# Row tiles of the first norm in groups of 2, 2, 4, 4, 4, the next group's rows between the matmul blocks, and two weight splits moved into the second norm

## The chip, the core and the metric

One core of one Trainium2 chip runs the whole kernel in one launch. The metric is the device time in microseconds (us). The engines named below are PE (TensorE, the matrix engine), DVE (VectorE), ACT (ScalarE), POOL (GpSimd) and SP (SyncE, which issues nearly all DMAs).

## The reference, cut to what matters

The reference is one decoder layer in float32 over 512 tokens of width 2048, conditioned on a vector `c`:

```python
mod = silu(c) @ w_ada + b_ada                    # 2048 -> 6 * 2048
shift1, scale1, gate1, shift2, scale2, gate2 = split(mod, 6)
h = rms_norm(x, norm1_g) * (1 + scale1) + shift1 # first norm
proj = h @ w_in                                  # retention, attention and indexer inputs
...                                              # retention heads, top-k sparse attention
x = x + gate1 * (concat(y_ret, y_dsa) @ w_out)
h = rms_norm(x, norm2_g) * (1 + scale2) + shift2 # second norm
y = square(relu(h @ w_mlp1)) @ w_mlp2            # 2048 -> 8192 -> 2048
return x + gate2 * y
```

## The kernel before

**Arithmetic.** Every float32 weight chunk is split in two: ACT writes the high part (`split_hi`, line 514), POOL subtracts it from the raw chunk and writes the low part (`split_lo`, line 739), and PE forms each product in three passes (high by high, high by low, low by high; line 1196). A split chunk lies in one of four places of `w_hi` and `w_lo`, and `split_hi` of a chunk waits until PE has used the chunk four before it. Raw weights come in units of four chunks into two slots of `raw`.

**Start.** `x` is 4 tiles of 128 tokens (1024 KB each), loaded into two places of `x_nat`. PE turns each tile (`turn_x`, 16 transposes), ACT copies the turned columns into `resid` and squares each `x` tile for the mean square (line 661). POOL takes the root, PE spreads it over the partitions (`spread`, line 1269), and DVE copies it to `rstd1` (line 842). Between its bursts PE does a few dummy matmuls (`fill`).

**Rows of the first norm.** The first norm needs scale and shift for each of the 16 row tiles (128 rows of the width 2048) of `h`. They come from `w_ada`, for which nothing is kept from call to call: for four row tiles there are 8 pieces of 1024 KB (`first_piece`, line 456; 4 pieces of scale, 4 of shift, each 128 partitions by 4 runs of 512 columns, so 2048 bytes in a run), loaded in turn into four buffers `first[0..3]`. A piece is issued on SP only when PE has used the piece four before it (`first_used`). PE multiplies each piece by the silu of `c` (`first_rows`, line 1283, 4 matmuls of 512 columns), accumulating in bank 3 of `pa`. When 8 pieces are in, ACT copies the bank to `part_rows` (`take_first`, line 520), PE sums and turns it (`sum_first`, line 1304), DVE adds the bias (line 817) and forms the gain (`fold`, line 822). Then, for each row tile: DVE writes `tmp` (line 830), ACT writes the high part of `h` (`h_high`, line 524), DVE the low part (line 834).

**Early chunks.** PE multiplies each row tile of `h` as soon as it is there with its 896 columns of `w_in` (`early_chunk`: four blocks into `pj`, one for each token tile, and three blocks into `pa`; 16 chunks in all). Groups are of four row tiles: group 0 is prepared ahead of the first chunk, and the pieces of group `cc` lie between the chunks of group `cc - 1`, none ahead of the first of them, four ahead of the second, two ahead of each of the others. The sum of group `cc` stands inside the fourth chunk, after its second block.

**SP's order.** SP works through one list: the constants, `x` tiles 0 and 1, the first four pieces, `x` tiles 2 and 3, the rest of group 0 with the four quarters of weight unit 0 (448 KB each), and then for each group 8 pieces with weight unit `cc` (1792 KB) after the fourth. A wait in this list holds back all that stands behind it.

**Second norm.** After the output projection the second norm writes 16 row tiles of `h` in the same three steps (`tmp` lies in `relu`, and the spread root stays in PSUM). PE starts `first_unit` (the first MLP unit, row tiles 0 to 7) as soon as its tiles come. ACT splits the chunks of the second MLP unit (`U_MLP + 1`) after it has written all 16 high parts.

Of the kernel before, what the change touches and what calls it, by code (L numbers as in the profile page):

```python
# [27 lines left out]
ALU = mybir.AluOpType  # L28
ACT = mybir.ActivationFunctionType

P = 128
# [68 lines left out]


def need(eng, sem, value):

    if isinstance(value, int) and value <= 0:
        return
    eng.wait_ge(sem, value)
# [20 lines left out]
def build(nc, x, vecs, b_ada, consts, w_ada, w_in, w_out, w_mlp1, w_mlp2, out):  # L127
# [21 lines left out]
    def small(name, *shape):  # L149
# [44 lines left out]

    x_nat = at("x_nat", 65536 + 16384, [P, 2, D])
    first = [at("ada_first0", 12 * 4096, [P, 2048]), at("ada_first1", 14 * 4096, [P, 2048]),
             at("ada_first2", RC + 4096, [P, 2048]), at("ada_first3", RC + 22528, [P, 2048])]
# [39 lines left out]
    x_turned, x_taken = sem("x_turned"), sem("x_taken")  # L237
    x_squared = sem("x_squared")
    rstd_spread = sem("rstd_spread")
# [117 lines left out]
    for n in range(2, ADA_PIECES):  # L357
        after = max(after, ada_place(n)[2] - 1)
        ADA_AFTER.setdefault(after, []).append(n)

    block = nc.Block()
    with block:
# [3 lines left out]
        def _(sp):  # L366
            def ada_piece(n):

                (sec, k), (b, _, freed) = divmod(n, 4), ada_place(n)
                if n == 0:  # L370
                    sp.wait_ge(first_used, 32)
# [21 lines left out]
            def load_head(k):  # L393

                g = k // 4
                if k == 0:
                    sp.wait_ge(mod_taken, 8 + ADA_SUMS)
                elif k == 1:
# [52 lines left out]
            def first_piece(cc, t):  # L451

                sec, s = divmod(t, 4)
                need(sp, first_used, 8 * cc + t - 3)
                col = D * (1 - sec) + 512 * cc
                sp.dma_start(first[t % 4][:].rearrange("p (k n) -> p k n", k=4),
                             ada_v[:, 4 * s:4 * s + 4, col:col + 512]).then_inc(first_landed[t % 4], 16)

# [6 lines left out]
            for s in range(2):  # L465
                sp.wait_ge(x_turned, 4 * s + 4)
                sp.wait_ge(x_squared, s + 1)
                sp.dma_start(x_nat[:, s, :], x[P * (s + 2):P * (s + 3), :]).then_inc(x_landed[s], 16)
            for t in range(4, 8):
                if t == 6:  # L470
                    load_quarter(0)
                first_piece(0, t)
            for j in range(1, 4):
                load_quarter(j)
            for cc in range(1, 4):
                for t in range(8):
                    if t == 4:
                        if cc == 1:
                            sp.wait_ge(x_turned, 16)
                            sp.wait_ge(x_squared, 4)  # L480
                        load_unit(cc)
                    first_piece(cc, t)
# [24 lines left out]
        def _(act):  # L507
# [8 lines left out]
            def take_first(cc):  # L516

                act.wait_ge(first_used, 8 * cc + 8)
                need(act, mod_summed, cc)
                act.activation(part_rows[:], pa[:, 3, :], ACT.Copy).then_inc(first_taken, 1)  # L520

# [133 lines left out]
            for tb in range(NB):  # L655
                if tb == 1:
                    act.wait_ge(rows_taken, 2)
                    act.activation(csilu[:, 1, :], vec[:, V_C:V_C + KT], ACT.Exp, scale=-1.0).then_inc(silu_exp, 1)
                act.wait_ge(x_landed[tb % 2], 16 * (tb // 2 + 1))
                need(act, x_squared, tb)  # L660
                act.activation(x_junk[:], x_nat[:, tb % 2, :], ACT.Square,
                               accum_out=ms[:, tb:tb + 1]).then_inc(x_squared, 1)
                for q in range(4):
                    act.wait_ge(x_turned, 4 * tb + q + 1)
                    act.activation(resid[:, 4 * q:4 * q + 4, P * tb:P * tb + P],
                                   pj[:, q, :].rearrange("p (k t) -> p k t", k=4), ACT.Copy).then_inc(x_taken, 1)
            for cc in range(4):
                for j in range(4):
                    if cc > 0 and j == 2:
                        take_first(cc)  # L670
                    split_hi(cc, j)
                    if cc == 0:
                        if j == 0:
                            take_first(0)
# [51 lines left out]

            mlp_step(0, 4)
            with act.Fori(1, STEPS - 1) as c:
# [51 lines left out]
        def _(dve):  # L780
            own = Steps(dve, dve_step)

            dve.memset(half[:], -0.5).then_inc(half_set, 1)
            own.step(dve.memset(c_wide[:], 0.0))
            dve.wait_ge(rows_turned, 1)
            dve.tensor_copy(bias_cols[:], pa[:, 0, 0:96]).then_inc(rows_taken, 1)
# [16 lines left out]
            def take_mod(n):  # L803

                col = 2 * KT + 4 * n
                dve.wait_ge(mod_summed, 4 + n + 1)
                summed = pj[:, 0, 0:4] if n in ADA_ASIDE else pa[:, 3, 0:4]
# [3 lines left out]
            def take_first_mods(cc):  # L811

                dve.wait_ge(mod_summed, cc + 1)
                sums_ = pa[:, 3, 0:8].rearrange("p (m sec) -> p sec m", sec=2)
                for sec in range(2):
                    col = KT * (1 - sec) + 4 * cc
                    dve.tensor_tensor(mod[:, col:col + 4], sums_[:, sec, :], bias_cols[:, col:col + 4],
                                      ALU.add).then_inc(mod_taken, 1)
# [17 lines left out]

            for cc in range(4):
                if cc == 0:
                    dve.wait_ge(x_squared, NB)
                    dve.tensor_scalar(ms[:, 0:NB], ms[:, 0:NB], 1.0 / D, EPS, ALU.mult, ALU.add).then_inc(ms_ready, 1)  # L840
# [4 lines left out]
                dve.wait_ge(mod_taken, 2 * cc + 2)  # L845
                fold(4 * cc, 0, KT, V_N1, 4)
                for m in range(5):
                    kt = 4 * cc + m
                    if m < 4:
                        modulate(kt, 0, resid, rstd1[:], tmp1, 0, t_ready, h_hi, h_ready, 0)  # L850
# [151 lines left out]
            def ada_add(n):  # L1002
# [5 lines left out]
                if n % 4 == 0:  # L1008
                    dve.wait_ge(mod_summed, max(4, 3 + n // 4))
                for i in range(4):  # L1010
# [10 lines left out]
            for q in range(Q_WO):  # L1021
# [35 lines left out]
                for n in ada_pieces_at(q):  # L1057
                    ada_add(n)
            dve.wait_ge(mod_taken, 8 + ADA_SUMS)
            fold(0, 1, 4 * KT, V_N2, KT)  # L1060
# [131 lines left out]
        def _(pe):  # L1192
# [85 lines left out]

            def silu_rows(src, s, sec):

                for i in range(4):
                    at_ = 32 * (4 * s + i) + 1 - sec
                    last = pe.matmul(pa[32 * i:32 * i + 32, 3, :], c_wide[:, at_:at_ + 32], src[i],  # L1283
                                     start=sec == 0 and s == 0, stop=sec == 1 and s == 3)
                return last

            def first_rows(cc, t):
# [8 lines left out]
                silu_rows([first[t % 4][:, 512 * i:512 * i + 512] for i in range(4)], s, sec).then_inc(first_used, 1)  # L1296

            def sum_first(cc):

                pe.wait_ge(first_taken, cc + 1)  # L1300
                if cc == 0:
                    pe.wait_ge(c_wide_ready, 2)
                for m in range(4):
# [21 lines left out]

# [24 lines left out]
            fill(10)  # L1350
            for cc in range(1, 5):
                for s in range(4):
                    if cc < 4:
                        for t in ((), (0, 1, 2, 3), (4, 5), (6, 7))[s]:
                            first_rows(cc, t)
                    early_chunk(4 * (cc - 1) + s, cc if cc < 4 and s == 3 else None)

            for j in range(4):
                pe.wait_ge(lo_done, Q_SMALL + j + 1)
                if j == 0:  # L1360
                    pe.wait_ge(mod_taken, 8)
                for kk in range(4):
# [17 lines left out]

            done = {"items": 0, "mods": 8, "bank3": 8, "heads": 0, "turns": 0}

# [344 lines left out]
```

## Time and profile before

| | |
|---|---|
| median of 3 runs | 2377.06 us (2375.36 to 2377.11) |
| time of the profiled execution | 2375.35 us |
| its span, first to last instruction | 2373.5 us |
| PE busy | 2343.3 us (99%) |
| granted TensorE clock, mean of the span | 0.998 |
| first early chunk starts | 44.99 us into the span |
| fifth early chunk (first of the second group) starts | 77.34 us |

All times of rows are microseconds from the start of the span. The share of the 16 DMA engines is that of the time in which they had a packet; a share near 1 means that the DMA never paused. The granted clock 1.00 is TensorE's upper level (2.4 GHz), 0.50 would be its lower one (1.2 GHz).

### The profile page before, as it was taken

What the parts mean: (1) busy time and instruction counts of PE and PEld (TensorE: products, weight loads), DVE (VectorE), ACT (ScalarE), POOL (GpSimd) and SP (SyncE); (2) the same over time, 40 slices, a digit from 0 to 9 for tenths busy, and PEclk for the clock granted to TensorE, in tenths of its full rate; (3) what the DMA queues carried; (4) which work ended last, traced back from release to release, by engine and by line L of the source; (5) the groups of instructions that cost most, each with busy time, mean ns of one, the idle gap of its engine ahead of it and who ended that gap; (6) DMA issues with size and microseconds to landing.
All of it is one profiled execution on the core that took longest, in us unless ns stands there. A gap on an engine that the chain in (4) does not pass through costs nothing.

```text
span 2373.5 us, 26660 instructions
## 1 busy us (share of the span) xinstructions
PE 2343.3 (99%) x10778; PEld 1902.1 (80%) x10778; DVE 964.1 (41%) x1360; ACT 644.1 (27%) x891; POOL 973.7 (41%) x414
## 2 busy tenths in 40 slices
PE   7999999999999999999999999999999999999999
PEld 4676688788878888788888888888888888888887
DVE  2249898877876877621121121121121121121121
ACT  4223332323224221321221221221221221221222
POOL 1343343344334334344444444444444444444442
PEclk9999999999999999999999999999999999999999
DMA  9976464578647423222333233223323322332231
GB/s 379 357 278 230 161 211 143 196 273 293 223 146 270 142 89 107 71 107 76 102 107 95 82 106 106 85 92 106 106 73 103 106 98 78 106 106 84 93 129 49
DMA packets 183985, 342.13 MB, mean 144 GB/s; under 512 B 4417, under 2 KB 31332, under 8 KB 183012
## 3 DMA queue, kind: packets, MB, share of 16 engines
q1 hardware_dynamic: 175280, 336.77, 41.4%
q10 hardware_dynamic: 8628, 4.28, 0.6%
q8 instruction: 55, 0.90, 0.2%
q14 instruction: 22, 0.18, 0.0%
HBM read 324.26 MB, written 16.78 MB: 144 GB/s over the span
## 4 chain that ended last, share of the span: by engine, by line
PE 93%; DVE 3%; DMA 2%; ACT 1%; issue 0%; SPq 0%; POOL 0%; ACTq 0%; DVEq 0%
PE pj L1196 56%; PE pa L1196 31%; DMA ada_first<-w_ada_in 2%; PE pa L1200 1%; PE pa L1283 1%; DVE part_rows L1015 1%; PE pa L1454 1%; PE pa L1413 1%; PE pa L1477 1%; DVE h L834 1%; PE pa L1276 1%; DVE relu L830 0%; PE pa L1534 0%; PE pa L1526 0%; DVE score L927 0%
## 5 line engine op out<-in xcount | busy, mean ns | idle before, releaser
L739 POOL TENSOR_TENSOR w_lo<-raw,w_hi 128x1024 fp32r<-128x1024 f32 (+1 forms) x396 | 954.5, 2412 | 1339.9 <-ACT w_hi L514 1339.8
L514 ACT ACTIVATE w_hi<-raw 128x1024 fp32r<-128x1024 f32 (+1 forms) x396 | 416.1, 1054 | 1491.2 <-PE pj L1196 945.7
L1196 PE MATMUL pj<-h,w_hi 128*128 128x512 f32 (+1 forms) x1696 | 526.0, 391 | 2.1 <-POOL w_lo L739 1.6
L1196 PE MATMUL pj<-w_hi,h 128*128 128x512 f32 x1408 | 454.1, 396 | 2.2 <-DVE h L834 1.1
L1196 PEld LDWEIGHTS pj<-h,w_hi 128*128 128x128 f32 (+1 forms) x1696 | 314.6, 187 | 74.5 <-issue 7.2
L1196 PE MATMUL pa<-h,w_hi 128*128 128x512 f32 x1152 | 354.9, 389 | 0.0
L1196 PE MATMUL pj<-h,w_lo 128*128 128x512 f32 (+1 forms) x848 | 330.2, 389 | 0.0
L1196 PEld LDWEIGHTS pj<-w_hi,h 128*128 128x128 f32 x1408 | 264.4, 188 | 74.4 <-issue 14.4
L1196 PE MATMUL pa<-mid,w_hi 128*128 128x512 f32 x1024 | 316.1, 390 | 0.0
L1196 PE MATMUL pj<-mid,w_hi 128*128 128x512 f32 x1024 | 315.8, 390 | 0.0
L1196 PE MATMUL pj<-w_lo,h 128*128 128x512 f32 x704 | 274.4, 390 | 0.0
L1196 PEld LDWEIGHTS pa<-h,w_hi 128*128 128x128 f32 x1152 | 216.2, 188 | 45.0
L1196 PE MATMUL pa<-h,w_lo 128*128 128x512 f32 x576 | 224.1, 389 | 0.0
L1196 PEld LDWEIGHTS pj<-mid,w_hi 128*128 128x128 f32 x1024 | 191.8, 188 | 39.6
L1196 PEld LDWEIGHTS pa<-mid,w_hi 128*128 128x128 f32 x1024 | 191.6, 188 | 39.5
L1196 PE MATMUL pa<-mid,w_lo 128*128 128x512 f32 x512 | 199.3, 389 | 0.0
L1196 PE MATMUL pj<-mid,w_lo 128*128 128x512 f32 x512 | 199.3, 389 | 0.0
L1196 PEld LDWEIGHTS pj<-h,w_lo 128*128 128x128 f32 (+1 forms) x848 | 158.5, 187 | 34.1
L1183 DVE SCALAR_TENSOR_TENSOR resid<-pa,mod,resid 128x512 f32<-128x512 f32 x64 | 48.1, 751 | 304.0 <-PE pa L1196 304.0
L1183 DVE SCALAR_TENSOR_TENSOR resid<-pj,mod,resid 128x512 f32<-128x512 f32 x64 | 47.5, 751 | 276.8 <-PE pj L1196 276.8
L1196 PEld LDWEIGHTS pj<-w_lo,h 128*128 128x128 f32 x704 | 132.3, 188 | 27.4 <-issue 1.7
L1015 DVE SCALAR_TENSOR_TENSOR ada_acc<-ada_rows,csilu,ada_acc 128x512 f32<-128x512 f32 x120 | 132.4, 1103 | 25.9 <-DMA ada_rows<-w_ada_in 22.0
(177 smaller groups left out, 1689.5 us busy)
## 6 DMA issues: line engine op xcount, KB each, us to landing
raw<-w_mlp_in SPq DMA_DIRECT2D x64, 2048.0 KB, 8.5
ada_rows<-w_ada_in SPq DMA_DIRECT2D x64, 1024.0 KB, 5.3
raw<-w_in_in SPq DMA_DIRECT2D x22, 2048.0 KB, 10.0
ada_first<-w_ada_in SPq DMA_DIRECT2D x32, 1024.0 KB, 10.9
raw<-w_out_in SPq DMA_DIRECT2D x8, 2048.0 KB, 8.6
ret<-ret_dram SPq DMA_DIRECT2D x32, 256.0 KB, 3.9
raw<-w_in_in SPq DMA_DIRECT2D x3, 1792.0 KB, 13.0
x_nat<-x_in SPq DMA_DIRECT2D x4, 1024.0 KB, 10.4
```

Source lines behind the costliest of these rows:

```text
L514: act.activation(split_chunk(w_hi, u, j), raw_chunk(u, j), ACT.Copy).then_inc(hi_done, 1)
L739: pool.tensor_tensor(split_chunk(w_lo, u, j), raw_chunk(u, j), split_chunk(w_hi, u, j).bitcast(F32), ALU.subtract).then_inc(lo_done, 1)
L834: dve.scalar_tensor_tensor(h[:, kt, LO, :], tmp[:, kt % 2, :], mod[:, shift_col + kt:shift_col + kt + 1], h[:, kt, HI, :].bitcast(F32), AL ...
L1015: last = dve.scalar_tensor_tensor(acc[:], ada_rows[b][:, i, :], c_col, acc[:], ALU.mult, ALU.add)
L1183: dve.scalar_tensor_tensor(resid[:, t, :], (pa if v % 2 else pj)[:, j, :], mod[:, 5 * KT + t:5 * KT + t + 1], resid[:, t, :], ALU.mult, AL ...
L1196: last = pe.matmul(dst, lhs[a], rhs[b], start=start and n == 0, stop=stop and n == 2)
L1200: return pe.transpose(dst, src, ident)
L1276: last = pe.matmul(bank[:, m:m + 1], rows[:, P * m:P * m + P], ones[:, 0:1], start=True, stop=True)
L1283: last = pe.matmul(pa[32 * i:32 * i + 32, 3, :], c_wide[:, at_:at_ + 32], src[i], start=sec == 0 and s == 0, stop=sec == 1 and s == 3)
L1413: pe.matmul(pa[:, n % 4, 0:span(i)], iqT[rows, hh // 2, P * i:P * i + P], ikT[rows, 0:span(i)], start=True, stop=True).then_inc(idx_done, 1)
L1454: last = pe.matmul(pa[:, bank, col:col + span(i)], qT[:, j, P * i:P * i + P], kT[:, g, 0:span(i)], start=True, stop=True)
L1477: last = pe.matmul(pa[:, 3, P * kb:], v_nat[:, kb, P * g:P * g + P], pT[:, PT_AT[kb]:PT_AT[kb] + width], start=kb == 0, stop=kb == NB - 1, ...
```

## The change

- The row tiles of the first norm come in five groups: tiles 0-1, 2-3, 4-7, 8-11, 12-15. Pieces of the two small groups have 256 columns (512 KB, runs of 1024 bytes); there are 40 pieces instead of 32, and the bytes are the same. The first buffer is another place from group 1 on.
- The 8 pieces of group 1 stand between the blocks of chunks 0 and 1, those of group 2 ahead of chunk 2 (two) and between the blocks of chunks 2 and 3 (six). Groups 3 and 4 stand as groups 2 and 3 stood.
- SP issues the quarters of unit 0 between the pieces of groups 0 and 1 (quarter 1 ahead of group 1, quarters 2 and 3 ahead of its pieces 6 and 7), and unit `cc - 1` inside group `cc` for `cc` of 2 to 4.
- DVE squares `x` tiles 1 and 3 (one `tensor_tensor_reduce` each), ACT tiles 0 and 2.
- ACT's order: for group 2, `take_first` comes ahead of the split of the second chunk of unit 1 (before: ahead of the third).
- In the second norm ACT splits the first two chunks of the second MLP unit after row tiles 11 and 13.

```diff
+GROUPS = ((0, 2), (2, 2), (4, 4), (8, 4), (12, 4))
+MODS = 2 * len(GROUPS)
...
+    def first_place(cc, t):
+        buffer = first_again if cc > 0 and t % 4 == 0 else first[t % 4]
+        return buffer[:, 0:4 * P * GROUPS[cc][1]].rearrange("p (k n) -> p k n", k=4)
...
                 need(sp, first_used, 8 * cc + t - 3)
-                col = D * (1 - sec) + 512 * cc
-                sp.dma_start(first[t % 4][:].rearrange("p (k n) -> p k n", k=4),
-                             ada_v[:, 4 * s:4 * s + 4, col:col + 512]).then_inc(first_landed[t % 4], 16)
+                col = D * (1 - sec) + P * GROUPS[cc][0]
+                sp.dma_start(first_place(cc, t),
+                             ada_v[:, 4 * s:4 * s + 4, col:col + P * GROUPS[cc][1]]).then_inc(first_landed[t % 4], 16)
...
                 sp.wait_ge(x_turned, 4 * s + 4)
-                sp.wait_ge(x_squared, s + 1)
+                sp.wait_ge((x_squared, x_squared_too)[s], 1)
...
-            for j in range(1, 4):
-                load_quarter(j)
-            for cc in range(1, 4):
+            load_quarter(1)
+            sp.wait_ge(x_squared, 2)
+            for t in range(8):
+                if t in (6, 7):
+                    load_quarter(t - 4)
+                first_piece(1, t)
+            sp.wait_ge(x_squared_too, 2)
+            sp.wait_ge(x_turned, 16)
+            for cc in range(2, 5):
                 for t in range(8):
                     if t == 4:
-                        if cc == 1:
-                            sp.wait_ge(x_turned, 16)
-                            sp.wait_ge(x_squared, 4)
-                        load_unit(cc)
+                        load_unit(cc - 1)
                     first_piece(cc, t)
...
-            for cc in range(4):
+            split_hi(0, 0)
+            take_first(0)
+            h_high(0)
+            split_hi(0, 1)
+            h_high(1)
+            split_hi(0, 2)
+            take_first(1)
+            h_high(2)
+            h_high(3)
+            split_hi(0, 3)
+            for cc in range(2, 5):
                 for j in range(4):
-                    if cc > 0 and j == 2:
+                    if j == (1 if cc == 2 else 2):
                         take_first(cc)
-                    split_hi(cc, j)
-                    if cc == 0:
-                        if j == 0:
-                            take_first(0)
-                        h_high(j)
-                    if cc > 0 and j == 2:
+                    split_hi(cc - 1, j)
+                    if j == 2:
                         for m in range(4):
-                            h_high(4 * cc + m)
+                            h_high(GROUPS[cc][0] + m)
...
                                bias=mod[:, 48 + kt:49 + kt]).then_inc(h2_hi, 1)
+                if kt in (11, 13):
+                    split_hi(U_MLP + 1, (kt - 11) // 2)
...
-            mlp_step(0, 4)
+            mlp_step(0, 6)
...
+            dve.wait_ge(x_landed[1], 16)
+            dve.tensor_tensor_reduce(x_junk2[:], x_nat[:, 1, :], x_nat[:, 1, :], 1.0, 0.0, ALU.mult, ALU.add,
+                                     ms[:, 1:2]).then_inc(x_squared_too, 1)
             dve.wait_ge(rows_turned, 1)
...
+            square_x(3)
+            for cc, (kt0, count) in enumerate(GROUPS):
...
-            def early_chunk(kt, group):
+            def early_chunk(kt, group, between={}):
...
+                    if tb in between:
+                        first_rows(*between[tb])
-                    if tb == 1 and group is not None:
+                    if tb == 1 and group is not None and not between:
                         sum_first(group)
                 for t in range(IQ_EARLY):
+                    if t == 0 and group is not None and between:
+                        sum_first(group)
...
+                    if NB + t in between:
+                        first_rows(*between[NB + t])
...
-            for cc in range(1, 5):
-                for s in range(4):
-                    if cc < 4:
-                        for t in ((), (0, 1, 2, 3), (4, 5), (6, 7))[s]:
-                            first_rows(cc, t)
-                    early_chunk(4 * (cc - 1) + s, cc if cc < 4 and s == 3 else None)
+            early_chunk(0, None, {n: (1, n) for n in range(6)})
+            early_chunk(1, 1, {0: (1, 6), 1: (1, 7)})
+            first_rows(2, 0)
+            first_rows(2, 1)
+            early_chunk(2, None, {1: (2, 2), 3: (2, 3), 5: (2, 4)})
+            early_chunk(3, 2, {0: (2, 5), 1: (2, 6), 2: (2, 7)})
+            for cc in range(3, 6):
+                for m in range(4):
+                    if cc < 5:
+                        for t in ((), (0, 1, 2, 3), (4, 5), (6, 7))[m]:
+                            first_rows(cc, t)
+                    early_chunk(4 * (cc - 2) + m, cc if cc < 5 and m == 3 else None)
```

## Rows read from the trace of the kernel before

**Rows 1.** The page: busy times, and the chain that ended last.
```profile
PE 2343.3 (99%) x10778; PEld 1902.1 (80%) x10778; DVE 964.1 (41%) x1360; ACT 644.1 (27%) x891; POOL 973.7 (41%) x414
...
PE 93%; DVE 3%; DMA 2%; ACT 1%; issue 0%; SPq 0%; POOL 0%; ACTq 0%; DVEq 0%
```

**Rows 2.** PE's waits, whole span: total us, times, longest.
```profile
PE pa L1283 <- DMA ada_first<-w_ada_in: 8.9, 8, 1.6
...
PE pj L1196 <- POOL w_lo L739: 1.6, 1, 1.6
```

**Rows 3.** Stretches: length, busy PE, PEld, DVE, ACT, POOL, clock, DMA share, GB/s.
```profile
0.00:60.00 60.00, 42.08 (x258) 27.72 (x258) 14.66 (x25) 25.63 (x37) 12.02 (x10) 0.91 1.00 379
10.00:20.00 10.00, 5.90 (x46) 2.75 (x44) 1.71 (x10) 5.22 (x9) 0.00 (x0) 1.00 1.06 393
20.00:30.00 10.00, 7.18 (x33) 5.45 (x34) 0.00 (x0) 5.02 (x7) 0.00 (x0) 0.53 1.02 402
...
60.00:70.00 10.00, 7.76 (x45) 4.47 (x49) 0.00 (x0) 0.40 (x1) 3.07 (x2) 1.00 1.05 387
```

**Rows 4.** The chain of waits, 39 to 80 us: start, us, what.
```profile
39.20 1.11 PE pa L1283 x8
...
44.99 3.02 PE pj L1196 x12
...
51.96 11.30 DMA ada_first<-w_ada_in
...
71.25 1.60 PE pj L1196 x6
72.85 0.80 PE pa L1304 x8
...
77.34 2.79 PE pj L1196 x11
```

**Rows 5.** Single microseconds of the stretches view, two places.
```profile
84.00:85.00 1.00, 1.00 (x16) 0.34 (x12) 0.00 (x0) 0.89 (x1) 0.00 (x0) 1.00 0.58 90
...
775.50:776.50 1.00, 1.00 (x11) 1.00 (x11) 0.29 (x1) 1.00 (x2) 0.05 (x1) 1.00 1.10 311
```

**Rows 6.** Timeline of SP: the issue after that pause.
```profile
83.45 0.37 SPq L456 DMA_DIRECT2D ada_first<-w_ada_in  x1
```

**Rows 7.** Timeline of PE, two pieces of group 0.
```profile
13.65 1.07 PE L1283 MATMUL pa<-ada_first,c_wide 128*32 128x512 f32 x8
...
21.07 1.93 PE L1283 MATMUL pa<-ada_first,c_wide 128*32 128x512 f32 x8 [1.64 <-DMA ada_first<-w_ada_in]
```

**Rows 8.** Timelines of ACT, POOL and DVE, 45 to 75 us.
```profile
71.31 0.60 ACT L520 ACTIVATE part_rows<-pa 128x512 f32<-128x512 f32 x1 [10.91 <-PE pa L1283]
71.81 0.95 ACT L514 ACTIVATE w_hi<-raw 128x896 fp32r<-128x896 f32 x1
...
45.06 7.68 POOL L739 TENSOR_TENSOR w_lo<-raw,w_hi 128x896 fp32r<-128x896 f32 x3 [8.19 <-ACT w_hi L514]
...
72.83 2.10 POOL L739 TENSOR_TENSOR w_lo<-raw,w_hi 128x896 fp32r<-128x896 f32 x1 [9.76 <-ACT w_hi L514]
...
48.30 2.50 DVE L830 SCALAR_TENSOR_TENSOR tmp<-resid,gain,rstd 128x512 f32<-128x512 f32 x1
...
73.94 1.01 DVE L822 SCALAR_TENSOR_TENSOR gain<-mod,vec 128x4 f32<-128x4 f32 x1
```

**Rows 9.** Second norm: timelines of ACT and DVE, then the chain.
```profile
980.69 0.72 ACT L687 ACTIVATE h<-relu,mod 128x512 fp32r<-128x512 f32 x1 [0.72 <-DVE relu L830]
...
986.35 1.63 DVE L834 SCALAR_TENSOR_TENSOR h<-relu,mod,h 128x512 fp32r<-128x512 f32 x2
...
987.10 1.05 ACT w_hi L514
...
988.23 2.38 POOL w_lo L739
...
990.65 9.36 PE pj L1196 x40
```

More of the change, by code:

```diff
@@ L195, in build @@
     x_nat = at("x_nat", 65536 + 16384, [P, 2, D])
+    x_junk2 = at("x_junk2", 8 * 4096, [P, D])
+    first_again = at("ada_first4", RC + 12288, [P, 2048])
     first = [at("ada_first0", 12 * 4096, [P, 2048]), at("ada_first1", 14 * 4096, [P, 2048]),
@@ L237, in build @@
     x_turned, x_taken = sem("x_turned"), sem("x_taken")
-    x_squared = sem("x_squared")
+    x_squared, x_squared_too = sem("x_squared"), sem("x_squared_too")
     rstd_spread = sem("rstd_spread")
@@ L370, in ada_piece @@
                 if n == 0:
-                    sp.wait_ge(first_used, 32)
+                    sp.wait_ge(first_used, 8 * len(GROUPS))
                 if n == ADA_EARLY[0]:
@@ L396, in load_head @@
                 if k == 0:
-                    sp.wait_ge(mod_taken, 8 + ADA_SUMS)
+                    sp.wait_ge(mod_taken, MODS + ADA_SUMS)
                 elif k == 1:
@@ L519, in take_first @@
                 need(act, mod_summed, cc)
-                act.activation(part_rows[:], pa[:, 3, :], ACT.Copy).then_inc(first_taken, 1)
+                width = P * GROUPS[cc][1]
+                act.activation(part_rows[:, 0:width], pa[:, 3, 0:width], ACT.Copy).then_inc(first_taken, 1)
             def h_high(kt):
@@ L659, in _ @@
                 act.wait_ge(x_landed[tb % 2], 16 * (tb // 2 + 1))
-                need(act, x_squared, tb)
-                act.activation(x_junk[:], x_nat[:, tb % 2, :], ACT.Square,
-                               accum_out=ms[:, tb:tb + 1]).then_inc(x_squared, 1)
+                if tb % 2 == 0:
+                    need(act, x_squared, tb // 2)
+                    act.activation(x_junk[:], x_nat[:, tb % 2, :], ACT.Square,
+                                   accum_out=ms[:, tb:tb + 1]).then_inc(x_squared, 1)
                 for q in range(4):
@@ L805, in take_mod @@
                 col = 2 * KT + 4 * n
-                dve.wait_ge(mod_summed, 4 + n + 1)
+                dve.wait_ge(mod_summed, len(GROUPS) + n + 1)
                 summed = pj[:, 0, 0:4] if n in ADA_ASIDE else pa[:, 3, 0:4]
@@ L813, in take_first_mods @@
                 dve.wait_ge(mod_summed, cc + 1)
-                sums_ = pa[:, 3, 0:8].rearrange("p (m sec) -> p sec m", sec=2)
+                kt0, count = GROUPS[cc]
+                sums_ = pa[:, 3, 0:2 * count].rearrange("p (m sec) -> p sec m", sec=2)
                 for sec in range(2):
-                    col = KT * (1 - sec) + 4 * cc
-                    dve.tensor_tensor(mod[:, col:col + 4], sums_[:, sec, :], bias_cols[:, col:col + 4],
+                    col = KT * (1 - sec) + kt0
+                    dve.tensor_tensor(mod[:, col:col + count], sums_[:, sec, :], bias_cols[:, col:col + count],
                                       ALU.add).then_inc(mod_taken, 1)
@@ L835, in modulate, with square_x @@
                                              h[:, kt, HI, :].bitcast(F32), ALU.add, ALU.subtract).then_inc(done, 1)
-            for cc in range(4):
+            def square_x(tb):
+                dve.wait_ge(x_landed[1], 16 * (tb // 2 + 1))
+                need(dve, x_squared_too, tb // 2)
+                dve.tensor_tensor_reduce(x_junk2[:], x_nat[:, 1, :], x_nat[:, 1, :], 1.0, 0.0, ALU.mult, ALU.add,
+                                         ms[:, tb:tb + 1]).then_inc(x_squared_too, 1)
+            square_x(3)
+            for cc, (kt0, count) in enumerate(GROUPS):
                 if cc == 0:
-                    dve.wait_ge(x_squared, NB)
+                    dve.wait_ge(x_squared, 2)
+                    dve.wait_ge(x_squared_too, 2)
                     dve.tensor_scalar(ms[:, 0:NB], ms[:, 0:NB], 1.0 / D, EPS, ALU.mult, ALU.add).then_inc(ms_ready, 1)
@@ L845, in _ @@
                 dve.wait_ge(mod_taken, 2 * cc + 2)
[L846 to L849, printed above, removed]
+                fold(kt0, 0, KT, V_N1, count)
+                for m in range(count + 1):
+                    kt = kt0 + m
+                    if m < count:
                         modulate(kt, 0, resid, rstd1[:], tmp1, 0, t_ready, h_hi, h_ready, 0)
@@ L1008, in ada_add @@
                 if n % 4 == 0:
-                    dve.wait_ge(mod_summed, max(4, 3 + n // 4))
+                    dve.wait_ge(mod_summed, max(len(GROUPS), len(GROUPS) - 1 + n // 4))
                 for i in range(4):
@@ L1058, in _ @@
                     ada_add(n)
-            dve.wait_ge(mod_taken, 8 + ADA_SUMS)
+            dve.wait_ge(mod_taken, MODS + ADA_SUMS)
             fold(0, 1, 4 * KT, V_N2, KT)
@@ L1277, in sum_mod @@
                 last.then_inc(mod_summed, 1)
[L1279 to L1285, printed above, removed]
             def first_rows(cc, t):
@@ L1295, in first_rows @@
                     need(pe, mod_taken, 2 * cc)
-                silu_rows([first[t % 4][:, 512 * i:512 * i + 512] for i in range(4)], s, sec).then_inc(first_used, 1)
+                for i in range(4):
+                    at_ = 32 * (4 * s + i) + 1 - sec
+                    last = pe.matmul(pa[32 * i:32 * i + 32, 3, 0:P * GROUPS[cc][1]], c_wide[:, at_:at_ + 32],
+                                     first_place(cc, t)[:, i, :], start=t == 0, stop=t == 7)
+                last.then_inc(first_used, 1)
             def sum_first(cc):
@@ L1302, in sum_first @@
                     pe.wait_ge(c_wide_ready, 2)
-                for m in range(4):
+                for m in range(GROUPS[cc][1]):
                     last = pe.matmul(pa[:, 3, 2 * m:2 * m + 2], part_rows[:, P * m:P * m + P], pick[:],
@@ L1360, in _ @@
                 if j == 0:
-                    pe.wait_ge(mod_taken, 8)
+                    pe.wait_ge(mod_taken, MODS)
                 for kk in range(4):
@@ L1379, in _ @@
                         last.then_inc(k_turned, 1)
-            done = {"items": 0, "mods": 8, "bank3": 8, "heads": 0, "turns": 0}
+            done = {"items": 0, "mods": MODS, "bank3": MODS, "heads": 0, "turns": 0}
             def bank3_free():
```

## The prediction

> **What bounds the kernel now.** I read the page first: PE is busy 99% of the span and is 93% of the chain that ended last [rows 1]. The kernel can gain only what PE waits, or lose by new waits. So PE's waits came second [rows 2]: of those that this change can touch, 8.9 us are for `ada_first` pieces, all in the first 65 us, and 1.6 us are one wait for `w_lo` in the second norm. Third, the stretches [rows 3]: the DMA share is 1.00 over the first 60 us and 1.05 over the next ten. The start is DMA-bound, at about 390 GB/s. Fourth, the chain around the early chunks [rows 4]: the first chunk starts at 44.99, the fifth at 77.34, and between them the chain lies on a landing (51.96 to 63.26). After that PE is never without work until the projections are done. What the first part of the change is worth is therefore read at one place: the start of the fifth chunk. Starting the first chunk early earns nothing if the fifth comes no earlier, as everything from there on is PE work that the change leaves alone.
>
> **Base.** The profiled execution took 2375.35 us, span 2373.5; the median of three is 2377.06, 1.71 above it. The sum below is a difference in the profiled execution, and I add it to the median.
>
> **Part 1: the bytes ahead of the fifth chunk.** It needs row tile 4, so pieces of 8 row tiles, all of `x`, four quarters and unit 1. That is constants and vectors 0.64 MB, `x` 4.19, pieces 16.78, quarters 1.84, unit 1 1.84: 25.28 MB. The change reorders these bytes and removes none: with groups of 2, 2, 4 the fifth chunk still waits for the third group's last piece, the same total. By [rows 3] 22.74 MB had moved at 60 us (379 GB/s) and 387 GB/s follow, so 25.28 MB are through at 66.6. The lag to the semaphore I take from the landing that ended at 63.26 [rows 4]: two pieces (2.10 MB) fewer, through at 61.1, so 2.2 us. Last landing: 68.8. Before, PE took that piece at 70.2 (71.25 less 1.07), so at most 1.4 us of lateness on this side can be won.
>
> **Part 2: 16 pieces with runs of 1024 bytes.** No row shows such runs. The nearest are 512-byte runs, 311 GB/s (loads of `ret`, 775.5 to 776.5 us) [rows 5], and 2048-byte runs, 390. One engine of 16 takes 26.3 ns for a run of 512 bytes and 84 ns for one of 2048; on the line between, 1024 bytes take 45.5 ns, 360 GB/s. The 8.39 MB then take 23.3 us instead of 21.5: +1.8. Bounds: 0, and 5.5 at 311 GB/s. I take 1.8. The Trainium skill ("DMA: Bandwidth & Descriptors", Specifications) puts the minimum for line rate at 512 bytes; by it this term is 0, and a rival below.
>
> **Part 3: a pause of the DMA queue.** The four buffers now hold half as much, 4 x 1.46 us of transfer. Piece 4 of group 1 may be issued only when piece 0 is used, and that now stands behind the first block of chunk 0; behind it in SP's list wait pieces 5 to 7, two quarters, group 2 and unit 1. When is chunk 0? Its group's last piece is at 9.48 MB: 60 less 13.26/0.39 is 26.0, plus 0.9 for eight short-run pieces, plus 2.2: 29.1. PE takes it (half of 1.07, say 0.6), and the chain from there was 4.68 us (44.99 less 40.31 [rows 4]), now about 4.0 (half a bank copied, two sums instead of four): 33.7. But PE must first do `x` tiles 2 and 3, six of the eight pieces, `spread` and the fills, partly at the lower level of the clock: before, in 20 to 30 us it granted 0.53 [rows 3] after 5.9 busy us of the ten before, and a piece took 1.93 instead of 1.07 [rows 7]. The change makes those ten us emptier still. Two pieces, eight spread matmuls and the fills at half clock put chunk 0 at 36. Piece 4 is issued one block (0.75) and one piece (0.6) after chunk 0's start, and data move 1.3 us after an issue to an empty queue (issue 83.45 [rows 6], 90 GB/s in 84 to 85 [rows 5], about 0.25 us at full rate). So data again at 36.4 to 38.7. What was queued (quarter 1 and four pieces, 7.0 us after 26.9) ended at 33.9. The pause is 2.5 to 4.8; I take 3.7. It is not made up, since the queue is full from there to the fifth chunk. Last landing: L = 68.8 + 1.8 + 3.7 = 74.3.
>
> **Part 4: from L to the fifth chunk.** Before, ACT copied the bank (0.60) and then split one chunk; POOL's `w_lo` of it (72.83 to 74.93) held DVE's `gain` from 73.94 to 74.95, the 128x4 operation taking 1.01 us [rows 8]. Earlier, with three `w_lo` in a row, DVE's 0.75 us `tmp` took 2.50: each DVE operation gets in only between two of POOL's. The new order for group 2 puts two splits behind `take_first`, the second and third chunk of unit 1, and both are ready (unit 1 lands some 10 us earlier, chunk 2 is used). So: piece 1.1, copy to L+1.7, first `w_lo` L+2.7 to 4.8, second to 6.9. PE sums until L+2.6 (block 0.7, sum 0.80), DVE adds the biases until L+2.9, `gain` waits to L+4.8, `tmp` to the end of the second `w_lo` and ends at L+7.5; ACT 0.73, DVE's low part 0.76 and the hand-overs: L+9.1. If DVE slips in ahead of the first `w_lo`, its second `tmp` is held instead, and the low part is again at L+9.1. With one `w_lo`, as before, it is L+6.4. Fifth chunk: 83.4, against 77.34: +6.1. PE has work until about L+4.8 and waits 4.3.
>
> **Part 5: costed at nothing.** DVE's squares: `x` tile 3 lands near 22.5, its square (under 3 us) and the root are done by 27, before the last piece of group 0; without that cover each us delays chunk 0 and adds to the pause. DVE's first square delays the silu chain by some 0.8 us; the first pieces, landed by 16, are buffered behind `x` tiles 2 and 3. Groups 3 and 4 have the order that 2 and 3 had, under PE work.
>
> **Part 6: second norm.** PE waited 1.6 us [rows 2] until 990.61, the end of `w_lo` [rows 9], so it was free at 989.05. The first unit's bank 0 was complete 12 products earlier (three matmuls each, 40 of them in 9.36 us, so 0.70), at 980.6; row tile 11's high part ended at 981.41. The split follows at once (1.05), `w_lo` (2.4) ends by 985: the wait goes, -1.6. The new `w_lo` can hold DVE's low parts, up to 2 x 2.4 us in all; PE needs the last row tile seven products after 989.05, at 993.9, and it was there at 988.0 [rows 9]. Covered, with 1 us over.
>
> **Sum.** +6.1 - 1.6 = +4.5: 2381.6 us. About 0.2% (4.75 us) is what a measurement of this kernel can tell from no change, so the forecast is no change by a hair. Its own range, with the pause of 2.5 to 4.8 and the short-run term of 1 to 2.5, is +2.5 to +6.5.
>
> **Rivals.**
> - *The clock falls at the new wait* (ends slower). Before, it fell after a stretch of 5.9 busy us in ten; here some ten us around the fifth chunk have 4.3 us of wait in one piece, and the wait for piece 4 of group 2 behind unit 1 is as long. Against: 7.76 busy us in 60 to 70 held it at 1.00 [rows 3]. If it falls for ten us from the fifth chunk on, PE-bound work loses 5 us: +9.5, 2386.6. It decides as soon as the low level lasts over 0.5 us there. The Trainium skill ("TensorE: Matmul & The Clock Gate", section "HAM oscillation — how this bites in real kernels") has the engine throttled again by waits between groups of matmuls. Chance 0.2.
> - *Short runs cost nothing, and the pause is at its low end.* L = 71.3 to 72.5: +1.5 to +2.7. This is where the skill's line-rate rule leads. For it: 512-byte loads still reach 311. Chance 0.24.
> - *The change does what an earlier first chunk suggests.* No pause, no cost of short runs, only one `w_lo` in the way: fifth chunk at 68.8 + 6.4 = 75.2, -2.1, with the norm -3.7: 2373.4. This is the floor: more than 0.2% cannot come out of PE's waits. Chance 0.1.
> - *The second norm gives nothing* (DVE held by `w_lo` past the 1 us over): +6.1. Chance 0.04.
>
> The forecast itself has 0.42, a bit over half of it under +4.75. Faster by over 0.2%: 0.03, kept for a fault in the argument. Same: 0.23 + 0.24 + 0.08 = 0.55 or a little less, 0.54. Slower: 0.19 + 0.2 + 0.04 = 0.43. The range that leaves out no more than 2 in 10 goes from just above the floor to the clock rival: 2375.5 to 2387.
>
> **What the profile after would show.** First chunk at 34 to 36; a stretch near 34 to 38 with DMA share under 0.5; PE waiting some 4 us for `ada_first` inside chunk 2; `gain` or `tmp` of row tile 4 at 2 us or more beside two `w_lo`; fifth chunk at 82 to 85; no wait for `w_lo` near the second norm. The prediction is wrong if the fifth chunk starts before 78, if the clock's row around it is under 1.00, or if waits appear after it.

## The result, and the profile after

The changed kernel takes 2384.08 us (median of 7 runs, 2382.72 to 2385.44), the kernel before on the same chip 2377.02 (7 runs): 7.06 us more, a ratio of 1.003 with a 95% interval of 1.002 to 1.004. That is slower by more than the 0.2% (4.75 us) that the prediction took as the least that can be told from no change, to which it had given 0.54 against 0.43 for slower. It lies inside the stated range (2375.5 to 2387.0), 2.5 us above the forecast of 2381.6, and above the forecast's own range (+2.5 to +6.5). The profiled execution took 2385.44 us (span 2383.7), the slowest of its seven, while the one of before (2375.35) is the fastest of its own: differences between the two profiles are some 3 us larger than that of the medians.

The page after, busy times and the chain:

```profile
PE 2350.7 (99%) x10842; PEld 1904.5 (80%) x10842; DVE 959.8 (40%) x1367; ACT 640.6 (27%) x888; POOL 974.7 (41%) x414
...
PE 94%; DVE 3%; DMA 2%; ACT 0%; issue 0%; SPq 0%; POOL 0%; ACTq 0%; DVEq 0%
```

It shows next to nothing, as in [rows 1]. PE's waits (total, times, longest) do:

```profile
PE pa L1327 <- DMA ada_first<-w_ada_in: 9.0, 6, 4.9
PE pj L1233 <- DVE h L862: 5.3, 5, 3.9
```

The waits for pieces are as long in sum as in [rows 2], but one of them is 4.9 us. A wait for `h` of 3.9 us is new, and the one for `w_lo` is gone. The stretches, with columns as in [rows 3]:

```profile
0.00:60.00 60.00, 44.94 (x325) 29.57 (x326) 15.51 (x32) 20.73 (x32) 9.59 (x9) 0.97 0.95 333
...
24.00:34.00 10.00, 9.21 (x89) 6.90 (x88) 3.36 (x9) 3.66 (x8) 3.10 (x2) 1.00 1.08 357
34.00:38.00 4.00, 3.40 (x26) 1.56 (x26) 2.83 (x2) 1.53 (x3) 2.10 (x1) 1.00 0.24 69
...
60.00:70.00 10.00, 5.09 (x26) 1.55 (x24) 0.00 (x0) 0.95 (x1) 2.07 (x1) 0.85 1.04 391
70.00:80.00 10.00, 10.00 (x48) 4.84 (x49) 0.07 (x1) 1.81 (x3) 0.30 (x1) 0.81 1.03 367
80.00:90.00 10.00, 6.07 (x19) 4.49 (x18) 9.33 (x11) 4.13 (x6) 4.00 (x3) 0.71 0.97 375
```

By 60 us 60 x 333 = 19.98 MB had moved instead of 22.74, 2.76 MB or 7.1 us of transfer less. From 34 to 38 us the DMA engines were nearly idle (0.24). Just ahead, with a share of 1.08, they moved 357 GB/s and not 390. The granted clock is below 1.00 around the fifth chunk (0.81 and 0.71 over the two stretches of ten us). The chain of waits, against [rows 4]:

```profile
34.92 0.98 PE pj L1233 x3
...
55.47 12.50 DMA ada_first<-w_ada_in
...
68.02 1.93 PE pa L1327 x8
...
77.13 0.99 PE pa L1327 x8
...
79.01 0.90 PE pa L1337 x8
...
80.20 1.65 DVE gain L850
...
81.88 2.54 DVE tmp L858
...
86.00 5.29 PE pj L1233 x12
...
95.27 8.25 DMA ada_first<-w_ada_in
...
117.58 3.01 PE pj L1233 x12
```

POOL's timeline:

```profile
79.70 4.15 POOL L763 TENSOR_TENSOR w_lo<-raw,w_hi 128x896 fp32r<-128x896 f32 x2 [11.53 <-ACT w_hi L528]
```

The first chunk starts at 34.92, ten us earlier than before; the fifth starts at 86.00, 8.7 us later than its 77.34. `gain` takes 1.65 us and `tmp` 2.54 beside two `w_lo` of POOL that run from 79.70 to 83.85. The fifth chunk's first 12 matmuls take 5.29 us, with the clock at its lower level; the last row is the ninth chunk's start. Between the two the chain lies on a landing again: PE stood idle for 0.65 us until it took that piece of group 3 at 103.57. The kernel before has no wait for a piece behind its fifth chunk.

### The profile page after: what moved, and what is told of

Read it like the earlier page. It is cut to its first block, busy times and chain, and to the rows that moved or that the text cites. A ratio compares the mean times of both kernels' runs of the same rounds, so it can differ in the third digit from the quotient of the medians.

```text
span 2383.7 us, 26806 instructions
## 1 busy us (share of the span) xinstructions
PE 2350.7 (99%) x10842; PEld 1904.5 (80%) x10842; DVE 959.8 (40%) x1367; ACT 640.6 (27%) x888; POOL 974.7 (41%) x414
## 4 chain that ended last, share of the span: by engine, by line
PE 94%; DVE 3%; DMA 2%; ACT 0%; issue 0%; SPq 0%; POOL 0%; ACTq 0%; DVEq 0%
PE pj L1233 57%; PE pa L1233 31%; DMA ada_first<-w_ada_in 2%; PE pa L1237 1%; PE pa L1327 1%; DVE part_rows L1052 1%; PE pa L1499 1%; PE pa L1458 1%; PE pa L1522 1%; PE pa L1313 1%; DMA rows<-vecs 0%; PE pa L1579 0%; PE pa L1571 0%; DVE score L964 0%; DVE ada_acc L1052 0%
```

## The experiments

Each was timed beside the kernel before on its own chip (2376.88 to 2376.98 us); the differences below are between medians. Differences to the changed kernel compare medians taken on different occasions, between which the kernel before moved by 0.14 us at most. L514 and the like are lines of each kernel's own file.

**1. The second-norm edit alone**, on the kernel before:

```diff
+                if kt in (11, 13):
+                    split_hi(U_MLP + 1, (kt - 11) // 2)
...
-            mlp_step(0, 4)
+            mlp_step(0, 6)
```

> The kernel before with the second-norm edit alone. Theory (terms add up): PE's wait of 1.6 us for w_lo near 989 us is gone, nothing else moves, 1.6 us faster than before. Rival (the new w_lo holds DVE in the norm, so the wait only changes its name): within 0.5 us of before, with a new wait of PE for h of 1 to 2 us.

Measured: 2375.07 against 2376.88, -1.8 us; the interval of the ratio, 0.9986 to 1.0004, includes 1, so the time alone doesn't prove it. The trace does: no wait for `w_lo` is listed, and the stretch that held it has a busy PE throughout (9.04 of 10 us before):

```profile
980.00:990.00 10.00, 10.00 (x46) 8.29 (x45) 9.82 (x11) 5.41 (x7) 5.08 (x2) 1.00 0.00 0
```

**2. The first-norm part alone**: the changed kernel with those two places undone.

> The changed kernel with the second-norm edit undone. Theory: 1.6 us slower than the changed kernel, so about 8.7 us over before, with the wait of 1.6 us for w_lo back. Rival: the same time as the changed kernel, 7 us over before.

Measured: 2386.33, +9.4 over before and 2.2 over the changed kernel, with the wait of 1.6 us for `w_lo` back. Both parts act as they did in the sum: one gives about 2 us, the other costs about 9.

This run has the first norm of the changed kernel, and its profiled execution (2384.15) is the fastest of its five, as that of before is the fastest of its own. So these two profiles compare better than the two in the section on the result. Its chain, from piece 4 of group 2 to the ninth chunk:

```profile
66.45 1.93 PE pa L1325 x8
...
83.94 4.61 PE pj L1231 x12
...
92.51 7.90 DMA ada_first<-w_ada_in
...
114.47 3.01 PE pj L1231 x12
```

The ninth chunk in the chain of the kernel before:

```profile
105.78 3.06 PE pj L1196 x12
```

The fifth chunk is 6.6 us late (83.94 against 77.34) and the ninth 8.7. The span is 8.9 us longer (2382.4 against 2373.5), so nearly all of the loss has arisen by the ninth chunk, and 2.1 us of it come after the start of the fifth: 1.6 in its first 12 matmuls (4.61 us instead of 3.01) and the rest around a piece for which PE waited 0.3 us.

**3. One `w_lo` instead of two beside the fifth chunk's chain**: in the changed kernel,

```diff
-                    if j == (1 if cc == 2 else 2):
+                    if j == 2:
                         take_first(cc)
```

> The changed kernel with ACT splitting the second chunk of unit 1 ahead of take_first of group 2, so that one w_lo instead of two meets DVE's gain and tmp. Theory (w_lo holds DVE): the fifth chunk starts 2.1 to 2.7 us earlier than 86.0, PE's wait for h falls from 3.9 to under 2 us, the clock does not fall there, and the time is 3 to 6 us under the changed kernel, +1 to +4 over before. Rival (the fall of the clock comes from the wait for pieces alone, the order of splits is hidden): fifth chunk within 0.5 us of 86.0, time within 1 us of the changed kernel.

Measured: 2380.96, +4.1 over before, 3.1 under the changed kernel. POOL's timeline in this kernel:

```profile
66.18 4.12 POOL L763 TENSOR_TENSOR w_lo<-raw,w_hi 128x896 fp32r<-128x896 f32 x2 [8.18 <-ACT w_hi L528]
79.64 2.12 POOL L763 TENSOR_TENSOR w_lo<-raw,w_hi 128x896 fp32r<-128x896 f32 x1 [9.35 <-ACT w_hi L528]
```

Its chain of waits (start, us, what):

```profile
80.14 1.65 DVE gain L850
...
81.82 0.76 DVE tmp L858
...
84.16 4.59 PE pj L1233 x12
```

The first two splits now lie at 66 us, where DVE has nothing to do. `gain` is still held by the third, `tmp` no longer: 0.76 instead of 2.54, and the fifth chunk comes 1.8 us earlier, a little less than the stated 2.1 to 2.7. PE's wait for `h` fell from 3.9 to 2.1. The profiled execution (2383.69) is the slowest of its ten, so the trace shows less of the gain than the medians. The clock fell all the same (4.59 us for 12 matmuls), which the expectation had denied; that part of it was wrong.

**4. No wait of group 1's pieces for chunk 0**: a piece of 256 columns fills half a buffer, so the first four pieces of group 1 take the other halves, with semaphores of their own.

```diff
+        at_ = 1024 if cc == 1 and t < 4 else 0
...
-                need(sp, first_used, 8 * cc + t - 3)
+                need(sp, first_used, (t + 1 if t > 4 else 0) if cc == 1 else 8 * cc + t - 3)
```

> The changed kernel with pieces 0 to 3 of group 1 in the unused second halves of the four buffers, so that no piece of group 1 waits for chunk 0. Theory (pause of the DMA queue): the stretch of 34 to 38 us without DMA is gone or under 1 us, the wait inside chunk 2 falls from 4.9 to 1 to 2 us, the clock does not fall at 67 us, the fifth chunk starts 3 to 5 us earlier than 86.0, and the time is +1 to +4 over before. Rival (the queue is slow because of the short runs, the pause only uncovers it): the last landing of group 2 moves by under 1 us, fifth chunk within 1 us of 86.0.

Measured: 2381.19, +4.3 over before, 2.9 under the changed kernel. The stretches of this kernel:

```profile
34.00:38.00 4.00, 3.40 (x27) 1.57 (x26) 2.86 (x3) 1.57 (x3) 2.12 (x1) 1.00 1.10 356
60.00:70.00 10.00, 5.47 (x25) 2.17 (x25) 0.00 (x0) 0.95 (x1) 2.07 (x1) 0.83 1.05 389
```

Its chain, at the fifth chunk:

```profile
81.73 4.40 PE pj L1235 x12
```

The DMA's share in 34 to 38 us is 1.10 instead of 0.24, and the fifth chunk starts 4.3 us earlier, as stated (3 to 5); the time is just above the stated +1 to +4. The long wait in chunk 2 is still 4.5 us, not 1 to 2: PE got there earlier as well, so the wait moved instead of shrinking, and the clock fell in it as before (0.83).

**5. The price of short runs by itself**: the kernel before, each of the 16 pieces of groups 0 and 1 as two DMAs.

```diff
+                width = 256 if cc < 2 else 512
+                for at_ in range(0, 512, width):
...
-                pe.wait_ge(first_landed[t % 4], 16 * (2 * cc + sec + 1))
+                uses = 2 * cc + sec + 1
+                pe.wait_ge(first_landed[t % 4], 16 * (uses + min(uses, 4)))
```

> The kernel before with each of the 16 pieces of its groups 0 and 1 loaded as two DMAs of 256 columns (runs of 1024 bytes), all else as it was: the price of short runs by itself, on 16.8 MB, twice the changed kernel's volume. Theory (a share of 1.1 at about 350 GB/s in the changed kernel's trace): 350 to 360 GB/s in 30 to 60 us instead of 390, the last landing of group 1 comes 3.5 to 5 us later, the fifth chunk 2.5 to 4 us later than 77.34, the time +2.5 to +4 over before. Rival (runs of 512 bytes and more move at full rate): 390 GB/s and within 0.5 us of before.

Measured: 2381.66, +4.7 over before (ratio 1.0009 to 1.0028), above the stated 2.5 to 4. The stretches of this kernel:

```profile
34.00:38.00 4.00, 2.82 (x22) 1.79 (x22) 0.69 (x1) 0.95 (x2) 1.54 (x1) 1.00 1.10 351
60.00:70.00 10.00, 6.53 (x32) 3.47 (x31) 0.00 (x0) 1.90 (x2) 4.12 (x2) 0.90 1.10 349
```

Its chain, at the fifth chunk:

```profile
82.93 3.01 PE pj L1198 x12
```

With all engines busy (share 1.10) runs of 1024 bytes move at 350 GB/s. 16.8 MB then take 4.9 us longer than at 390, less the 1.4 by which PE was late before: 3.5. The fifth chunk is 5.6 late. Most of the rest goes with a clock of 0.90 in 60 to 70 us: one chunk's first 12 matmuls took 4.29 us there instead of 2.99. The waits for pieces are longer (13.5 us in sum, the longest 2.0, against 8.9 and 1.6); that they let the clock fall is argued, not shown. The edit also halves the size of each DMA, as the change does, and this run does not separate that from the length of the runs.

**6. Dummy matmuls in the wait ahead of the fifth chunk**, on the changed kernel:

```diff
             early_chunk(3, 2, {0: (2, 5), 1: (2, 6), 2: (2, 7)})
+            pe.wait_ge(mod_taken, 6)
+            fill(24, pa[:, 3, P:2 * P])
```

> The changed kernel with 24 dummy matmuls (3.2 us) on PE in its wait between the fourth and the fifth chunk. Theory (the clock falls because of this wait and the fall costs time of its own): the clock stays at 1.00 from 84 to 90 us, the first 12 matmuls of the fifth chunk take 3.0 us instead of 5.3, and the time is 2 to 3 us under the changed kernel, +4 to +5 over before. Rival (the fall comes from the whole low activity since 60 us, or costs nothing): clock as before the edit, time within 1 us of the changed kernel.

A stretch of this kernel:

```profile
80.00:90.00 10.00, 10.00 (x70) 8.86 (x69) 7.22 (x8) 3.68 (x5) 3.79 (x2) 1.00 0.85 324
```

Its chain, at the fifth chunk:

```profile
85.26 2.77 PE pj L1233 x12
```

Timelines of DVE and PE in this kernel, at the same place:

```profile
83.02 0.75 DVE L862 SCALAR_TENSOR_TENSOR h<-tmp,mod,h 128x512 fp32r<-128x512 f32 x1
...
79.74 5.52 PE L1378 MATMUL pa<-con 128*128 128x128 f32 x48
85.01 0.47 PE L1233 MATMUL pj<-w_hi,h 128*128 128x512 f32 x1
```

The clock stayed at 1.00 and the 12 matmuls took 3.0 us (85.01 to 88.02) instead of 5.29: with this wait filled, the fall is gone. Yet the fill was too long. DVE had written the row tile at 83.77, but the 24 dummy matmuls, meant for 3.2 us, took 5.3 and kept PE until 85.01, so the chunk began about 1.2 us later than it could. Of the 2.3 us that the lower clock cost the 12 matmuls, this edit could give back about 1.1, and not the stated 2 to 3. The median is 2383.48, 0.6 us under the changed kernel, and its interval (1.0017 to 1.0036 of before) holds the changed kernel's: no gain that can be told, but no sign that the fall is cheap either. Averaged over the span the granted clock was 0.996 in six of the changed kernel's seven executions and 0.997 in the other; it was 0.997 to 0.999 in nine of these ten. So the lower clock was most likely in the median run too, and not only in the profiled one.

**7 and 8. Edits 3 and 4 together, without and with ten dummy matmuls.**

> The changed kernel with both earlier edits: pieces of group 1 ahead, and one w_lo instead of two beside gain and tmp. Theory (terms add up): the fifth chunk starts near 79.7 us (81.7 with the first edit alone, 2.0 for the second), the time is +0.5 to +2.5 over before. Rival (each edit removes the same wait): fifth chunk at 81 to 82, +4 over before.

> As the kernel with both edits, plus 10 dummy matmuls (1.3 us) in the wait ahead of the fifth chunk. Theory: the clock stays at 1.00 there, 1 to 2 us under the kernel with both edits, within 1.5 us of before; it would show that what is left over before is the price of short runs. Rival: no difference to the kernel with both edits, or slower by up to 1.3 us.

Measured: 2378.26 (+1.3, ratio 0.9994 to 1.0014) and 2377.73 (+0.8, 0.999 to 1.001). The first is 5.8 us under the changed kernel, and the single edits gave 3.1 and 2.9: they add up. The median is as the theory had it (+0.5 to +2.5). In the profile, though, the fifth chunk started at 81.44: not near 79.7, but where the rival put it (81 to 82). This execution granted 0.74 instead of 0.84 (experiment 4) in 20 to 30 us, began its first chunk 0.8 us later and took piece 4 of group 2 1.5 us later (66.13 against 64.65); that the one led to the other is not shown. The fill again gives half a microsecond that can't be told from none. It says nothing on the price of the clock: in the profile without it the clock was already at 1.00 from 70 to 90 us, and the fifth chunk's 12 matmuls took 3.01 us.

**9 and 10. Groups of four with full runs, only the order mended**, on the kernel before (9 with the second-norm edit, 10 without):

```diff
+            early_chunk(0, None)
+            for t in range(4):
+                first_rows(1, t)
+            early_chunk(1, None)
+            early_chunk(2, None, {3: (1, 4), 5: (1, 5)})
+            early_chunk(3, 1, {0: (1, 6), 1: (1, 7)}, sum_at=2)
...
                     split_hi(cc, j)
+                    if cc == 1 and j == 2:
+                        take_first(cc)
```

> Groups of four with 2048-byte runs as before, but the pieces 4 to 7 of group 1 stand between the blocks of chunks 2 and 3, the sum comes after the third block of chunk 3, ACT splits the third chunk of unit 1 ahead of take_first of group 1, and the second-norm edit is in. Theory (the fifth chunk is bound by the last landing near 68.8 us plus a chain of about 6 us that w_lo must not touch): no w_lo beside gain, fifth chunk at 74.4 to 75.5 instead of 77.34, 2 to 2.9 us, plus 1.6 to 1.8 from the norm: 3.5 to 4.7 us faster than before. Rival (PE's waits only move, or the clock falls in another place): fifth chunk at 77 or later, and no more than the 1.8 us of the norm edit alone.

> The same without the second-norm edit. Theory: 2 to 2.9 us faster than before. Rival: within 0.5 us of before.

Measured: 2371.47 and 2374.16 against 2376.98: 5.5 us faster (ratio 0.9978, 0.9969 to 0.9987) and 2.8 us faster (0.9983, 0.9974 to 0.9993). Both did better than or as stated (3.5 to 4.7, and 2 to 2.9). The kernel of experiment 9 beats the kernel before and the changed one, and it passes the 2373.4 that the prediction called the floor. Of its PE waits:

```profile
PE pa L1287 <- DMA ada_first<-w_ada_in: 5.1, 5, 1.6
```

POOL's timeline:

```profile
67.54 2.10 POOL L743 TENSOR_TENSOR w_lo<-raw,w_hi 128x896 fp32r<-128x896 f32 x1 [4.50 <-ACT w_hi L514]
```

The chain, from the sum of group 1 to the fifth chunk:

```profile
70.95 0.88 PE pa L1308 x8
...
74.68 3.05 PE pj L1200 x12
```

No `w_lo` runs between 69.64 and 78.54, so nothing holds `gain` and `tmp`, and the fifth chunk starts at 74.68, 2.7 us ahead of before. Waits for pieces fell from 8.9 to 5.1 us in sum, with chunk 2 on PE while pieces 4 and 5 come.

## Why the prediction came out as it did

**What bounds the start: right.** The first chunk came ten us earlier and the time rose; what counts in the main is the fifth chunk. That all behind it would be left alone was wrong, as told below.

**Part 1, the bytes and 1.4 us to win: right.** Experiments 9 and 10 took that and the blocked 0.85 us of `gain` with the first chunk where it was (44.77 in experiment 9). The 2373.4 of the prediction is thus no floor for this start: it left one `w_lo` in the way, which experiment 9 removed, and counted only 1.6 us for the second norm.

**Part 2, short runs: the right mechanism, under-sized.** The line between 512 and 2048 bytes gave 360 GB/s and 1.8 us. Measured are 350 (experiment 5), so 8.39 MB cost 24.0 - 21.5 = 2.5 us; at the 357 of the changed kernel's own stretch it would be 2.0. The Trainium skill's minimum of 512 bytes for line rate ("DMA: Bandwidth & Descriptors", Specifications) does not hold here: at twice that size a tenth of the rate was missing at full engine share. The measurement decides.

**Part 3, the pause: right.** Taken at 3.7 us, it was 3.0 of the four us from 34 to 38, plus a slow restart (241 GB/s in the next three, at a share of 0.81). Removing it gave 2.9 us. The forecast had the ten us of 20 to 30 emptier than before and chunk 0 at up to 36; PE was busy for 9.7 of them instead of 7.2, the clock was 0.87 and not 0.53, and chunk 0 came at 34.9. All losses of transfer together were forecast at 5.5 us. They were 7.1 in the changed kernel's own profile, that of its longest execution, and 6.2 in that of experiment 2 (339 GB/s over the first 60 us). Piece 4 of group 2, forecast near 66.2 (8.1 us before the last landing), was taken at 68.0 in the first and at 66.45 in the second.

**Part 4, two `w_lo`: right.** From the end of the last piece (78.12) to the fifth chunk it took 7.9 us; forecast were 8.0 (9.1 less 1.1). Experiment 2 has 7.9 too. Experiment 3 took one away, worth 3.1 us. That one engine waits for the other here is a rule of the Trainium skill ("SBUF — State Buffer", SBUF: two separate sides): a DVE operation with two SBUF inputs and a GpSimd operation that reads SBUF exclude each other for the whole instruction. The trace agrees, and in the second norm it shows the rule's other side. POOL's timeline of the changed kernel:

```profile
994.46 2.59 POOL L763 TENSOR_TENSOR w_lo<-raw,w_hi 128x1024 fp32r<-128x1024 f32 x1 [19.12 <-ACT w_hi L528]
997.35 2.51 POOL L763 TENSOR_TENSOR w_lo<-raw,w_hi 128x1024 fp32r<-128x1024 f32 x1 [0.31 <-ACT w_hi L528]
```

DVE's, in the same microseconds:

```profile
995.48 2.11 DVE L862 SCALAR_TENSOR_TENSOR h<-relu,mod,h 128x512 fp32r<-128x512 f32 x1
997.63 0.75 DVE L858 SCALAR_TENSOR_TENSOR relu<-resid,gain,pa 128x512 f32<-128x512 f32 x1
```

The operation with both inputs in SBUF is held (2.11), the one that reads `pa`, in PSUM, runs at 0.75 beside a `w_lo`.

**Part 5, at nothing: right.** DVE's second square ended at 24.7, ahead of group 0's last piece at 30.3.

**Part 6, the second norm: right.** -1.6 was forecast; -1.8, -2.2 and -2.7 (experiment 9 against 10) were measured; the two `w_lo` cost DVE 2.7 us (two operations of 2.1 instead of 0.75) and PE did not wait.

**What the sum left out: the time after the fifth chunk.** The prediction had it that everything from there on is PE work that the change leaves alone. Experiment 2 shows 2.1 us lost there, 1.6 of them by the lower clock in the first 12 matmuls and the rest around a wait for a piece of group 3. In the changed kernel's own profile it is 3.1 us (the ninth chunk is 11.8 us late, the fifth 8.7): 2.3 by the clock, and the rest around the 0.65 us of wait at 103.57. For that wait the prediction had no term. The fall of the clock it had as a rival with a chance of 0.2, at 5 us for ten us of lower clock; it came, at 1.6 to 2.3 us behind the start of the fifth chunk. Of the three signs by which the prediction would call itself wrong, two are there: the clock's row around the fifth chunk is 0.71, and a wait has appeared after it. The third is not, as the chunk starts at 86.0 and not before 78.

The clock fell in 60 to 70 us in every profiled variant with groups of 2, 2, 4, 4, 4. In the changed kernel's profile it was low first in the 4.9 us wait of chunk 2, where the piece behind it took 1.93 us instead of 1.07. As an estimate, that cost 1.0 us ahead of the fifth chunk, as PE took the last piece at 77.13 and not at 76.1 (68.0 and three pieces of 1.05 MB at 390 GB/s). Then came the second fall, ahead of the fifth chunk. The Trainium skill's rule that waits between groups of matmuls throttle the engine again ("TensorE: Matmul & The Clock Gate", HAM oscillation — how this bites in real kernels) fits.

**The account.** From the profiles: +6.6 at the fifth chunk (experiment 2; forecast 6.1), +2.1 after it (forecast nothing), -1.8 in the second norm (experiment 1; forecast 1.6), together +6.9 where the medians say +7.1. So the terms of the forecast were each near what was measured, and the missing 2.5 us are for the most part the time after the fifth chunk. That the result still lies inside the stated range is owed to the clock rival, which set its upper end; the forecast's own range, whose upper end works out at +6.3 and not +6.5, was missed.

From the medians: +7.1 = 5.8 (pause and second `w_lo` together, experiment 7; singly 2.9 and 3.1) + 1.3 left over; the 1.3 holds about -2 of the norm, so 3.3 are short runs and what goes with them. The forecast's terms for the same were 3.7, 2.7, -1.6 and 1.8, less the 2.1 us between the bytes' floor and the fifth chunk of before. The clock's cost is spread over these terms. What stays open is how the half microsecond at the fifth chunk divides between the rate of short runs, the slow restart and the clock, and what the clock alone costs the median run: experiment 6 held it up, but took back half of the gain by its own length.

## What to carry to other kernels

Where a start is bound by the bytes that a later stage needs, a finer first group gave nothing here: find the first point that all later work hangs on, and ask whether fewer bytes or a shorter chain stand ahead of it. Half-sized pieces in the same number of buffers halve the cover of the DMA queue, and a consumer that is now busy between pieces releases them late; use the freed halves. Keep GpSimd's two-input work off the few microseconds in which VectorE's two-input operations are the chain; moving one split ahead of them gave 1.8 us at the fifth chunk and about 3 us by the medians. Follow a forecast past the point at which it is read: here a quarter of the loss arose behind it. And before dummy work is used to fill a wait, check its length against the wait, or it costs what it was to save.

## What the runs showed of the hardware that I had not expected

- Loads with runs of 1024 bytes moved at 349 to 351 GB/s with all engines busy (share 1.10, experiment 5), those with 2048 at 390 [rows 3], with 512 at 311 [rows 5]: for 1024 some 10 GB/s less than a straight line in time per run gives.
- Waits of 4.5 to 5.7 us inside otherwise steady matmul work went with a fall of the clock in each of the seven profiles that had one (0.68 to 0.86 in 60 to 70 us), while in the kernel before, with waits of up to 1.6 us in 50 to 64 us, it stayed at 1.00. In experiment 5, with no wait for a piece over 2.0 us, it was 0.90.
